# Modulation's products move from TensorE to VectorE, with its weights transposed and its tiles spread further along the stream

## The chip, the cores and the metric

One core of a Trainium2 chip runs the whole program as one launch. The metric is the device time of that launch in microseconds (us). It has five engines with a queue each: TensorE (PE; its weight loads are listed as PEld), VectorE (DVE), ScalarE (ACT), GpSimd (POOL) and SyncE (SP), which here only issues DMAs.

## The reference, cut to what matters

Two transformer blocks run one after the other on 256 tokens of width 2048, all in float32. What the change touches is the adaptive modulation of the first block:

```
mod   = silu(c)     @ ada_w + ada_b        # ada_w: 2048 x 12288, c: one vector of 2048
mod_c = silu(c_ctx) @ ada_w + ada_b
sh1, sc1, g1, sh2, sc2, g2 = split(mod, 6)  # 2048 each
sh1c, sc1c, ...            = split(mod_c, 6)
z  = modulate(rmsnorm(x,  norm1_g), sh1,  sc1)  @ w_in
zc = modulate(rmsnorm(xc, norm1_g), sh1c, sc1c) @ w_in
x  = x + g1 * (concat(attn, rwkv) @ w_out)
x  = x + g2 * swiglu(modulate(rmsnorm(x, norm2_g), sh2, sc2), ffn_w1, ffn_w3, ffn_w2)
```

Of `mod_c` only its first third (shift 1 and scale 1) reaches the output. The second block projects a memory of 256 rows with `mem_n @ w_mem_kv`, 2048 to 2048 columns, twice; that product depends on nothing of the first block.

## The kernel before, in words

**One stream of weights.** Every weight matrix is cut into tiles of 512 rows by 256 columns, 512 KB each, laid on 128 partitions as 1024 values a row. `weight_stream` (L58) lists all tiles in the order in which they are used, 1016 of them "split" tiles and 192 "raw" tiles of modulation. SyncE (L2624 to L2636) loads tile j into slot j modulo 6 of the ring `raw`, once tile j-6 has been used up, in order.

**Split tiles.** A float32 product is made of three products of halves. ScalarE rounds the tile (`hi`, L1462); then `hi` is subtracted from the tile (`lo`) by VectorE for even tiles (L1946) and by GpSimd for odd ones (L2535). Both go to `whl`, a ring of 4 slots, free again when TensorE has multiplied the tile four places back. `split_ahead` (L425) queues these steps up to 3 tiles of the stream ahead of TensorE, raw tiles counted. TensorE multiplies at L992.

**Modulation.** Column group `nt` (48 of them, 256 columns each) takes 4 raw tiles. Both vectors, silu(c) and silu(c_ctx), stand in `sc16`, each column 16 times over, as stationary operand of 32 columns; TensorE streams the raw tile past it, 4 matmuls a tile, in float32 (L944, `ada_tile`; the profile counts 8 each, two per matmul). The sums lie on 128 PSUM partitions; ScalarE copies them to `part`, TensorE adds them and turns them with two small matmuls (L952, `ada_sum`), and VectorE adds the bias into `mod`. So one `mod` column holds one output column on each partition.

**The order.** `schedule` (L326) is the same program for all engines, each of which queues its own part: memory's first norm beside 16 raw tiles; memory's 64 split tiles with one raw tile behind each (`memory_kv`; products of `mem0`, `mem1`), beside the sums of squares of context and x; the norms of x and of the context; then `w_k`, `w_v` (16 tiles each), `w_wa`, `w_ka`, `w_va`, `w_q` (4 each of the first three, 4 of the last) with 3 or 2 raw tiles behind each; from there on no raw tile is left. Then come attention, the RWKV scan, `w_out`, the feed-forward part in three parts of 8, 8 and 6 steps j with 8 split tiles (`ffn1`, `ffn3`) each, and the second block. The norms need modulation's groups 0 to 15, `w_out` needs 16 to 23, the second norm 24 to 39, `ffn2` 40 to 47. Within a queue everything is in order; semaphores link the queues.

## Time and profile before

| what | value |
|---|---|
| median of 3 runs | 4066.92 us (4062.89 to 4071.34) |
| the profiled execution, its own time | 4049.6 us |
| its span, first to last instruction | 4047.8 us |
| granted TensorE clock, mean | 0.982 |
| PE busy | 3859.6 us (95%) |
| VectorE busy | 1772.3 us (44%) |
| GpSimd busy | 1373.7 us (34%) |
| modulation on TensorE (L944) | 1536 matmuls, 113.8 us busy, from 16.6 to 641 us |

The profile lists instructions by line, engine and shape with their busy time, the mean of one in ns, and the idle time in front of them with what ended it. A timeline row starts with the start time and the duration in us of a run of like instructions; "x8" is their count. Matmul ends are modelled, so the distance between two starts says more than the duration. PEclk is the granted clock, 1.0 at 2.4 GHz, 0.5 at 1.2 GHz. The rows come further down.

### The profile page before, as it was taken

What the parts mean: (1) busy time and instruction counts of PE and PEld (TensorE: products, weight loads), DVE (VectorE), ACT (ScalarE), POOL (GpSimd) and SP (SyncE); (2) the same over time, 40 slices, a digit from 0 to 9 for tenths busy, and PEclk for the clock granted to TensorE, in tenths of its full rate; (3) what the DMA queues carried; (4) which work ended last, traced back from release to release, by engine and by line L of the source; (5) the groups of instructions that cost most, each with busy time, mean ns of one, the idle gap of its engine ahead of it and who ended that gap; (6) DMA issues with size and microseconds to landing.
All of it is one profiled execution on the core that took longest, in us unless ns stands there. A gap on an engine that the chain in (4) does not pass through costs nothing.

```text
span 4047.8 us, 81819 instructions
## 1 busy us (share of the span) xinstructions
PE 3859.6 (95%) x35588; PEld 3337.7 (82%) x35588; DVE 1772.3 (44%) x2247; ACT 1597.6 (39%) x2028; POOL 1373.7 (34%) x632
## 2 busy tenths in 40 slices
PE   8999999989888899999998999999899999999998
PEld 5777777888886778888887888897788888888887
DVE  2242125566664664344445445435333443333443
ACT  3342224622112344444444444434344444444443
POOL 2331113100001345455453344444343334443343
PEclk9999999999999999999999999999899999999999
DMA  8887665100001445555553554454455555555543
GB/s 325 285 306 255 234 220 181 51 22 4 4 4 66 152 161 192 192 188 191 184 197 134 180 176 171 163 166 159 163 184 174 174 169 175 177 175 173 173 161 136
DMA packets 183124, 667.53 MB, mean 165 GB/s; under 512 B 20432, under 2 KB 20432, under 8 KB 182384
## 3 DMA queue, kind: packets, MB, share of 16 engines
q1 hardware_dynamic: 176544, 642.07, 46.8%
q10 hardware_dynamic: 4944, 16.03, 1.1%
q8 instruction: 283, 4.64, 0.4%
q0 software_dynamic: 1280, 4.20, 0.3%
q14 instruction: 73, 0.60, 0.0%
HBM read 653.82 MB, written 8.39 MB: 164 GB/s over the span
## 4 chain that ended last, share of the span: by engine, by line
PE 86%; DVE 4%; ACT 3%; issue 2%; DMA 2%; PEld 1%; POOL 1%; ACTq 0%; PEldq 0%; DVEq 0%; POOLq 0%; SPq 0%
PE ps L992 68%; PE ps L944 2%; PE ps L1236 2%; PE ps L1212 2%; PE ps L1148 1%; PE ps L1226 1%; PEld ps L992 1%; ACT whl L1462 1%; POOL whl L2535 1%; DVE whl L1946 1%; PE ps L1450 1%; PE ps L1434 1%; PE ps L1337 1%; PE ps L923 1%; DMA raw<-in_w_k 1%
## 5 line engine op out<-in xcount | busy, mean ns | idle before, releaser
L992 PE MATMUL ps<-halves,whl 128*128 128x256 f32 (+1 forms) x14752 | 2594.7, 336 | 62.9 <-POOL halves L2535 17.9
L992 PEld LDWEIGHTS ps<-halves,whl 128*128 128x128 f32 x14752 | 2241.8, 191 | 384.1 <-issue 87.1
L2535 POOL TENSOR_TENSOR whl<-raw,whl 128x1024 fp32r<-128x1024 f32 x508 | 1241.3, 2444 | 1849.1 <-ACT whl L1462 1849.0
L1462 ACT ACTIVATE whl<-raw 128x1024 fp32r<-128x1024 f32 x1016 | 1062.3, 1055 | 1096.3 <-PE ps L992 748.8
L1946 DVE TENSOR_TENSOR whl<-raw,whl 128x1024 fp32r<-128x1024 f32 x508 | 792.7, 1561 | 1380.2 <-ACT whl L1462 1379.9
L992 PE MATMUL ps<-whl,halves 128*128 128x256 f32 x2752 | 488.8, 336 | 0.1
L992 PEld LDWEIGHTS ps<-whl,halves 128*128 128x128 f32 x2752 | 416.7, 188 | 63.1 <-issue 9.2
L1462 ACT ACTIVATE work<-ps 128x512 f32<-128x512 f32 (+1 forms) x240 | 131.5, 550 | 295.4 <-PE ps L992 225.7
L2535 POOL TENSOR_TENSOR halves<-mix,halves 128x1024 fp32r<-128x1024 f32 (+1 forms) x16 | 27.7, 1736 | 549.5 <-ACT halves L1462 549.5
L1946 DVE TENSOR_TENSOR work<-work,ps 128x512 f32<-128x512 f32 x157 | 107.7, 686 | 128.3 <-ACT work L1462 127.5
L944 PE MATMUL ps<-raw,sc 128*32 128x256 f32 x1536 | 113.8, 393 | 2.9 <-DMA raw<-in_ada 2.9
L1212 PE MATMUL ps<-X,BT 64*64 64x64 f32 x2560 | 94.3, 220 | 5.0 <-issue 4.8
L1236 PE MATMUL ps<-Xt,T 64*64 64x32 f32 x2560 | 93.1, 219 | 3.5 <-issue 3.2
L1212 PEld LDWEIGHTS ps<-X,BT 64*64 64x64 f32 x2560 | 85.7, 136 | 8.6 <-issue 7.2
L1236 PEld LDWEIGHTS ps<-Xt,T 64*64 64x64 f32 x2560 | 85.7, 135 | 5.3 <-issue 4.0
L1462 ACT ACTIVATE xw<-xw,cols 128x384 f32<-128x384 f32 (+1 forms) x32 | 25.0, 780 | 150.0 <-DVE cols L1952 150.0
L1946 DVE TENSOR_TENSOR T<-ps,rwc 128x512 f32<-128x512 f32 x80 | 55.1, 688 | 59.0 <-PE ps L1212 59.0
L1226 PE MATMUL ps<-T,Xt 64*64 64x32 f32 x2048 | 73.5, 218 | 4.1 <-issue 3.9
L1462 ACT ACTIVATE work<-x 128x512 f32<-128x512 f32 (+1 forms) x40 | 28.8, 719 | 121.6 <-DVE x L1949 63.3
L1226 PEld LDWEIGHTS ps<-T,Xt 64*64 64x64 f32 x2048 | 69.2, 135 | 8.9 <-issue 7.5
L944 PEld LDWEIGHTS ps<-raw,sc 128*32 128x32 f32 x1536 | 35.9, 109 | 45.0 <-issue 31.3
L1462 ACT ACTIVATE R<-ps 128x1024 f32<-128x1024 f32 x8 | 8.2, 1025 | 159.1 <-PE ps L1258 135.9
(248 smaller groups left out, 2450.1 us busy)
## 6 DMA issues: line engine op xcount, KB each, us to landing
raw<-in_ffn SPq DMA_DIRECT2D x264, 512.0 KB, 4.3
raw<-in_ada SPq DMA_DIRECT2D x192, 512.0 KB, 4.6
raw<-in_w_kv SPq DMA_DIRECT2D x192, 512.0 KB, 3.6
raw<-in_w_in_b SPq DMA_DIRECT2D x160, 512.0 KB, 3.6
raw<-in_w_in_a SPq DMA_DIRECT2D x128, 512.0 KB, 3.6
raw<-in_mem SPq DMA_DIRECT2D x64, 512.0 KB, 5.4
raw<-in_w_out_a SPq DMA_DIRECT2D x48, 512.0 KB, 3.8
raw<-in_w_out_b SPq DMA_DIRECT2D x48, 512.0 KB, 4.1
```

The lines of the kernel that those rows point to most:

```text
L923: m = self.e.matmul(self.X(2)[:, 0:T], self.ones, self.work4[q][:, c, :], start=(q == 0 and c == 0), stop=(q == 3 and c == 3))
L944: m = self.e.matmul(self.G(b)[32 * g:32 * g + 32, 0:256], self.sc16[:, 32 * k:32 * k + 32], raw[:, g, :], start=(t.kg == 0), stop=(t.kg == ...
L992: p = self.e.matmul(o, x, y, start=bi not in begun, stop=final and kc == 3 and m == len(pairs) - 1, skip_group_check=True)
L1148: m = self.e.matmul(o[h, s, c, :], lhs(r, s, d, c), rhs(r, s, d, c), start=True, stop=True)
L1212: m = self.e.matmul(o[h, c, :], q["BT"][h, s, c, :], q["X"][h, s, c, :], start=True, stop=True)
L1226: m = self.e.matmul(o[h, c, :], q["Xt"][h, s, c, :], self.even(T1[h, s, c, :], lv), start=True, stop=True)
L1236: m = self.e.matmul(o[h, c, :], T1[h, s, c, :], self.odd(q["Xt"][h, s, c, :], lv), start=True, stop=True)
L1337: m = self.e.matmul(self.X(0)[:, 0:T], self.ones, sq[:, c, :], start=(n == 0 and c == 0), stop=(n == 7 and c == 1), skip_group_check=True)
L1434: m = self.e.matmul(b[:, w * gi:w * gi + w], qs[gi][:, c, 128 * qb:128 * qb + 128], ks[gi][:, c, 0:w], start=True, stop=True)
L1462: return self.e.activation(out, in_, func, **kw)
L1946: return self.e.tensor_tensor(out, a, b, op)
L2535: return self.e.tensor_tensor(out, a, b, op)
```

## The change

Of the 48 column groups only 8 (the even ones of 0 to 15) stay on TensorE (`BY_PE`). The other 40 go to VectorE. For those, the host lays ada_w out transposed (`adaT`): a tile has 128 output columns on the partitions and 1024 rows of the reduction along the free axis. Both vectors are loaded spread over all partitions (`c_rows`, 1 MB each), ScalarE and VectorE make silu of them (`silu`), and VectorE multiplies a tile by the vector and sums along the row in one `scalar_tensor_tensor` with an accumulator output (`ada_rows`, L2095 of the changed kernel). Groups below 16 need it a second time for c_ctx (L2091). Two small additions finish a group (`ada_columns`).

The order changes too: 4 raw tiles, not 16, stand ahead of memory's first tile; memory's first 48 tiles have 5 raw tiles per 4, its last 16 have 1 each; behind `w_k` come 2 instead of 3, behind `w_wa`, `w_ka`, `w_va` 1 instead of 2; 32 raw tiles (groups 40 to 47) move into steps 1 to 7 of the feed-forward part, for which silu(c) is loaded and made a second time (`reload_x`, `silu(1)`). Groups of TensorE and VectorE alternate up to group 15.

```diff
+BY_PE = range(0, 16, 2)
+MODULATION = [0, 2, 4, 1, 6, 3, 8, 5, 10, 7, 12, 9, 14, 11, 13, 15, *range(16, 48)]
+BESIDE_MEM = (1, 1, 1, 2)
+BESIDE_NORM = (1, 1, 1, 1)
+BESIDE = (("w_k", range(1, 4), 2), ("w_v", range(4), 2), ("w_wa", range(1), 1), ("w_ka", range(1), 1), ("w_va", range(1), 1), ("w_q", range(1), 2))
+BESIDE_FFN = (0, 5, 5, 5, 5, 5, 5, 2)
-BESIDE_NORM = (3, 3, 3, 3)
-BESIDE = (("w_k", range(1, 4), 3), ("w_v", range(4), 2), ("w_wa", range(1), 2), ("w_ka", range(1), 2), ("w_va", range(1), 2), ("w_q", range(1), 2))
...
-    names.extend(itertools.islice(modulation, 16))
-    for w in [(f"mem{lay}", n, kg) for lay in range(2) for n in range(8) for kg in range(4)]:
-        names += [w, next(modulation)]
+    names.extend(itertools.islice(modulation, 4))
+    for i, w in enumerate((f"mem{lay}", n, kg) for lay in range(2) for n in range(8) for kg in range(4)):
+        names += [w, *itertools.islice(modulation, BESIDE_MEM[i % 4] if i < 48 else 1)]
...
-            add("ffn1", [j])
-            add("ffn3", [j])
+            beside = itertools.islice(modulation, BESIDE_FFN[j] if k0 == 0 else 0)
+            for w in [(name, j, kg) for name in ("ffn1", "ffn3") for kg in range(4)]:
+                names += [w, *itertools.islice(beside, 1)]
...
+    def silu(self, again):
+        for t in range(1 if again else 2):
+            self.wait_ge("ld_c2" if again else "ld_c", t)
+            if t:
+                self.wait_ge("silu_v", ("rows", 0))
+            self.act(self.silu_half[again], self.silu_in[t], ACT.Tanh, scale=0.5).then_inc(self.sig("silu_s", ("rows", t + 2 * again)), 1)
...
+    def silu(self, again):
+        for t in range(1 if again else 2):
+            x = self.silu_in[t]
+            self.wait_ge("silu_s", ("rows", t + 2 * again))
+            self.stt(x, self.silu_half[again], 1.0, x, ADD, MUL).then_inc(self.sig("silu_v", ("rows", t + 2 * again)), 1)
+
+    def ada_rows(self, t, i):
+        f, k = divmod(t.kg, 2)
+        raw, x = self.raw_of(t), self.silu_in[0]
+        self.wait_ge(f"raw{t.j % NRAW}", t.j)
+        if t.nt < 16:
+            self.wait_ge("silu_v", ("rows", 1))
+            self.e.scalar_tensor_tensor(self.silu_half[0][:, 0:1024], raw, 0.5, self.silu_in[1][:, 1024 * k:1024 * k + 1024], MUL, MUL,
+                                        accum_out=self.row_sums(i)[:, k, f, 1:2]).then_inc(self.own(), 1)
+            self.wait_own()
+        self.wait_ge("silu_v", ("rows", 2 if t.nt >= 40 else 0))
+        self.e.scalar_tensor_tensor(raw, raw, 0.5, x[:, 1024 * k:1024 * k + 1024], MUL, MUL,
+                                    accum_out=self.row_sums(i)[:, k, f, 0:1]).then_inc(self.sig("ada_v", t.a), 1)
+        self.last_row = t.a
+
+    def ada_columns(self, nt, i):
+        n = 2 if nt < 16 else 1
+        r = self.row_sums(i)[:, :, :, 0:n]
+        dst = self.mod[:, 4 * nt:4 * nt + 4].rearrange("p (f t) -> p f t", t=2)[:, :, 0:n]
+        b = self.cst("ada_b", 96)[:, 2 * nt:2 * nt + 2].unsqueeze(2).to_broadcast([128, 2, n])
+        self.wait_ge("ada_v", self.last_row)
+        self.tt(dst, r[:, 0], r[:, 1], ADD).then_inc(self.own(), 1)
+        self.wait_own()
+        self.tt(dst, dst, b, ADD).then_inc(self.sig("mod_v", nt), 1)
...
                 if old.kind == "raw":
-                    self.wait_ge("ada_mm", old.a)
+                    self.wait_ge("ada_mm" if old.name == "ada" else "ada_v", old.a)
```

What VectorE has queued, at three places. First, in memory's product, where a group that now belongs to VectorE passes. Before, `mod<-ps` adds a bias, `whl<-raw,whl` is the low half of a split tile, `work<-work,ps` collects a product of memory:

```order
L1946 TENSOR_TENSOR mod<-ps,const 128x4
L1946 TENSOR_TENSOR work<-work,ps 128x512
L1946 TENSOR_TENSOR whl<-raw,whl 128x1024 x2
L1946 TENSOR_TENSOR mod<-ps,const 128x4
L1946 TENSOR_TENSOR work<-work,ps 128x512
```

Now, for one such group (`c_70` is silu(c_ctx), `mix` silu(c), `ch` takes a product that nobody reads):

```order
L1997 TENSOR_TENSOR whl<-raw,whl 128x1024
L2091 SCALAR_TENSOR_TENSOR ch,cols<-raw,c_70 128x1024
L2095 SCALAR_TENSOR_TENSOR raw,cols<-raw,mix 128x1024
L2091 SCALAR_TENSOR_TENSOR ch,cols<-raw,c_70 128x1024
L2095 SCALAR_TENSOR_TENSOR raw,cols<-raw,mix 128x1024
L2091 SCALAR_TENSOR_TENSOR ch,cols<-raw,c_70 128x1024
L2095 SCALAR_TENSOR_TENSOR raw,cols<-raw,mix 128x1024
L1997 TENSOR_TENSOR mod<-ps,const 128x4
L1997 TENSOR_TENSOR whl<-raw,whl 128x1024
L2091 SCALAR_TENSOR_TENSOR ch,cols<-raw,c_70 128x1024
L2095 SCALAR_TENSOR_TENSOR raw,cols<-raw,mix 128x1024
L1997 TENSOR_TENSOR mod<-cols 128x4
```

Between two low halves stand up to six instructions of 1024 values where nothing of that size stood. Second, VectorE beside `w_v`, before:

```order
L1946 TENSOR_TENSOR whl<-raw,whl 128x1024
L1946 TENSOR_TENSOR mod<-ps,const 128x4
L1946 TENSOR_TENSOR whl<-raw,whl 128x1024
L1946 TENSOR_TENSOR mod<-ps,const 128x4
L1949 SCALAR_TENSOR_TENSOR vT<-ps,const,vT 128x2x255 x4
```

and now:

```order
L2095 SCALAR_TENSOR_TENSOR raw,cols<-raw,mix 128x1024 x2
L1997 TENSOR_TENSOR whl<-raw,whl 128x1024
L2095 SCALAR_TENSOR_TENSOR raw,cols<-raw,mix 128x1024 x2
L1997 TENSOR_TENSOR mod<-cols 128x2
L1997 TENSOR_TENSOR mod<-mod,const 128x2
L2000 SCALAR_TENSOR_TENSOR vT<-ps,const,vT 128x2x255 x4
```

Each tile of `w_v` brings two instructions of 1024 values along. Third, VectorE in the feed-forward part (the first rows are the gate's two steps and the low halves), before:

```order
L1946 TENSOR_TENSOR work<-work,ps 128x512
L1949 SCALAR_TENSOR_TENSOR work<-work 128x512
L1946 TENSOR_TENSOR whl<-raw,whl 128x1024 x2
L1946 TENSOR_TENSOR work<-work,ps 128x512
L1949 SCALAR_TENSOR_TENSOR work<-work 128x512
```

and now, in a step with 5 raw tiles:

```order
L1997 TENSOR_TENSOR work<-work,ps 128x512
L2000 SCALAR_TENSOR_TENSOR work<-work 128x512
L1997 TENSOR_TENSOR whl<-raw,whl 128x1024
L2095 SCALAR_TENSOR_TENSOR raw,cols<-raw,mix 128x1024
L1997 TENSOR_TENSOR whl<-raw,whl 128x1024
L1997 TENSOR_TENSOR work<-work,ps 128x512
L2000 SCALAR_TENSOR_TENSOR work<-work 128x512
L1997 TENSOR_TENSOR whl<-raw,whl 128x1024
L2095 SCALAR_TENSOR_TENSOR raw,cols<-raw,mix 128x1024 x2
```

They stand between the low halves on which TensorE waits.

## Rows read from the trace of the kernel before

**Rows 1.** The page, busy time by engine and in 40 slices

```profile
PE 3859.6 (95%) x35588; PEld 3337.7 (82%) x35588; DVE 1772.3 (44%) x2247; ACT 1597.6 (39%) x2028; POOL 1373.7 (34%) x632
```

**Rows 2.** Stretches: us, busy (count) by engine, PEclk, DMA share, GB/s

```profile
50.00:100.00 50.00, 50.00 (x344) 36.90 (x345) 10.93 (x14) 16.22 (x20) 17.04 (x10) 1.00 0.91 332
41.00:292.10 251.10, 250.45 (x1656) 186.97 (x1656) 68.36 (x99) 94.72 (x120) 84.27 (x47) 0.99 0.85 302
298.39:619.50 321.11, 318.35 (x2048) 233.88 (x2052) 75.00 (x116) 73.20 (x107) 53.95 (x24) 0.99 0.68 238
1482.20:1504.40 22.20, 22.20 (x130) 19.58 (x129) 10.70 (x8) 10.54 (x13) 11.44 (x5) 1.00 0.59 197
```

**Rows 3.** Timeline of PE, memory's product: four tiles, four raw tiles

```profile
199.92 0.61 PE L952 MATMUL ps<-const,work 128*128 128x2 f32 x4
200.39 3.03 PE L992 MATMUL ps<-halves,whl 128*128 128x256 f32 x16
203.34 0.64 PE L944 MATMUL ps<-raw,sc 128*32 128x256 f32 x8
203.91 3.09 PE L992 MATMUL ps<-halves,whl 128*128 128x256 f32 x16
...
214.60 0.61 PE L952 MATMUL ps<-const,work 128*128 128x2 f32 x4
```

**Rows 4.** Timeline of PE: memory's tiles 1, 3 and 49; w_k's first product

```profile
41.02 5.41 PE L992 MATMUL ps<-halves,whl 128*128 128x256 f32 x16 [3.08 <-issue]
...
50.47 3.05 PE L992 MATMUL ps<-halves,whl 128*128 128x256 f32 x16
...
234.38 3.03 PE L992 MATMUL ps<-whl,halves 128*128 128x256 f32 x16
...
298.39 7.32 PE L992 MATMUL ps<-halves,whl 128*128 128x512 f32 x24 [1.33 <-DVE halves L1949]
```

**Rows 5.** Timeline of PE: tiles of w_k, w_v, w_va, w_q

```profile
383.28 5.69 PE L992 MATMUL ps<-halves,whl 128*128 128x512 f32 x24 [0.32 <-POOL whl L2535]
391.00 5.76 PE L992 MATMUL ps<-halves,whl 128*128 128x512 f32 x24
...
449.79 5.74 PE L992 MATMUL ps<-halves,whl 128*128 128x512 f32 x24
455.46 1.07 PE L944 MATMUL ps<-raw,sc 128*32 128x256 f32 x16
...
598.86 6.01 PE L992 MATMUL ps<-whl,halves 128*128 128x256 f32 x48
...
643.43 4.63 PE L992 MATMUL ps<-halves,whl 128*128 128x256 f32 x24
```

**Rows 6.** VectorE's 1024-value instructions with two operands in SBUF: min/median/max ns

```profile
L1949 DVE SCALAR_TENSOR_TENSOR u<-u,Pinv x8: 1219/1221/1222, 835.2 to 1192.5; 128x1024 f32<-128x1024 f32 x8
```

**Rows 7.** Timeline: a low half on VectorE between two on GpSimd

```profile
1488.11 2.40 POOL L2535 TENSOR_TENSOR whl<-raw,whl 128x1024 fp32r<-128x1024 f32 x1
1488.78 2.81 DVE L1946 TENSOR_TENSOR whl<-raw,whl 128x1024 fp32r<-128x1024 f32 x1 [2.67 <-ACT whl L1462]
...
1490.87 2.98 POOL L2535 TENSOR_TENSOR whl<-raw,whl 128x1024 fp32r<-128x1024 f32 x1 [0.36 <-ACT whl L1462]
```

**Rows 8.** Groups by shape: a read of an accumulator, a table load, memory's collecting step

```profile
L1462 ACT ACTIVATION_READ_ACCUMULATOR hbl<-hbl,cols 128x1 f32 x32 | 6.1, 192 | 0.0
L1462 ACT ACT_TABLE_LOAD x24 | 30.8, 1283 | 1.2 <-PEq L2835 0.7
L1946 DVE TENSOR_TENSOR work<-work,ps x157: 670/687/691, 58.5 to 3859.7; 128x512 f32<-128x512 f32 x157
```

**Rows 9.** Timeline of ACT at the start; of VectorE before the feed-forward part

```profile
9.90 1.06 ACT L1462 ACTIVATE work<-hal 128x1024 f32<-128x1024 f32 x1 [0.21 <-DMA hal<-in_memT]
...
31.77 0.42 ACT L1462 ACTIVATE halves<-tm 128x256 fp32r<-128x256 f32 x1 [0.45 <-DVE tm L1949]
...
1431.02 1.75 DVE L1982 RECIPROCAL rst<-rst 128x256 f32<-128x256 f32 x1 [0.48 <-ACT rst L1462]
```

**Rows 10.** Stretch with the granted clock low, columns as in rows 2

```profile
41.00:47.00 6.00, 5.97 (x25) 4.53 (x25) 0.91 (x1) 2.40 (x3) 2.37 (x1) 0.56 0.90 363
```

More of the change, by code:

```diff
@@ L25 @@
     [f"raw{i}" for i in range(NRAW)]
[L26 to L27 removed]
+    + ["hi", "lo_v", "lo_g", "mm", "ada_mm", "ada_v"]
+    + [f"ld_mem{i}" for i in range(4)] + ["ld_const", "ld_c", "ld_c2", "ld_ctx", "ld_x", "ld_attn", "ld_rwkv", "ld_gup", "ld_x2", "ld_ret", "ld_x3", "ld_dil"]
     + ["ld_dec0", "ld_dec1", "st_x", "st_out"]
@@ L110, in weight_stream @@
     for j, (name, nt, kg) in enumerate(names):
-        kind = {"ada": "raw", "w_gd": "tail"}.get(name, "split")
+        kind = {"ada": "raw", "adaT": "raw", "w_gd": "tail"}.get(name, "split")
         out.append(Tile(j, name, nt, kg, 160 if name == "w_gd" else 256, kind, n, a))
@@ L329, in schedule @@
         rest(self.squares(0))
-        run_all((self.normed(0, 0, "HB"), 2), (limited(modulation, 16), 1))
+        run_all((self.normed(0, 0, "HB"), 5), (limited(modulation, 4), 1))
         for r in (None, 1, 2):
-            run_all((limited(memory, 16), 1), (limited(modulation, 16), 1), (self.squares(r) if r else iter(()), 1))
+            if not r:
+                self.silu(0)
+            run_all((self.after(limited(memory, 16), modulation, BESIDE_MEM), 1), (self.squares(r) if r else iter(()), 1))
         self.modulation()
@@ L369, in schedule @@
         self.root_of_sums(3)
+        self.silu(1)
         for part, (k0, k1) in enumerate(((0, 4), (4, 8), (8, 11))):
@@ L374, in schedule @@
                 if j:
-                    rest(chain(gate, value))
+                    run_all((chain(gate, value), 1), (limited(modulation, BESIDE_FFN[j] if part == 0 else 0), 1))
                 else:
@@ L403, in shift, with after, row_sums @@
         return {1: self.mods[:, 0, 1, :], 2: self.mods[:, 0, 0, :], 3: self.mods[:, 3, 0, :]}[k]
-    def ada_all(self):
-        for nt in range(48):
-            yield from self.ada(nt)
+    def after(self, g, other, counts):
+        counts = itertools.cycle(counts)
+        for _ in g:
+            rest(limited(other, next(counts)))
+            yield
+    def ada_all(self):
+        before = None
+        for i, nt in enumerate(MODULATION):
+            for kg in range(4):
+                if nt in BY_PE:
+                    t = self.next_tile("ada", BY_PE.index(nt), kg)
+                    self.ada_tile(t)
+                else:
+                    t = self.next_tile("adaT", nt, kg)
+                    self.ada_rows(t, i)
+                if before and kg == 0:
+                    self.ada_part(*before)
+                if before and kg == 2:
+                    self.ada_sum(before[0])
+                    before = None
+                if kg == 3:
+                    if nt in BY_PE:
+                        before = (nt, t.a)
+                    else:
+                        self.ada_columns(nt, i)
+                yield
+    def row_sums(self, i):
+        return self.cols[:, 8 * (i % 4):8 * (i % 4) + 8].rearrange("p (k f t) -> p k f t", k=2, f=2)
     def ev_lora(self, job):
@@ L438, in hi_lo @@
         return self.A("wh")[:, t.n % NW, 0:4 * t.w], self.A("wl")[:, t.n % NW, 0:4 * t.w]
-    def ada(self, nt):
-        for kg in range(4):
-            self.ada_tile(self.next_tile("ada", nt, kg))
-            if nt not in (0, 16) and kg == 0:
-                self.ada_part(nt - 1)
-            if nt not in (0, 16) and kg == 2:
-                self.ada_sum(nt - 1)
-            if nt in (15, 47) and kg == 3:
-                self.ada_part(nt)
-                self.ada_sum(nt)
-            yield
     def part(self, nt):
-        return self.parts[nt % 2]
+        return self.parts[nt // 2 % 2]
     def ada_bank(self, nt):
-        return (4, 5, 7)[nt % 3]
+        return (4, 5, 7)[nt // 2 % 3]
     def norm_tm(self, k, c):
@@ L2621, in schedule @@
                 self.e.dma_start(dst[:, 4 * q:4 * q + 4, :], io[src][:, 4 * q:4 * q + 4, :]).then_inc(self.sig(name, q, 16), 16)
+            if t.j == 6:
+                for i in range(2):
+                    self.e.dma_start(self.silu_in[i], io["c_rows"][i]).then_inc(self.sig("ld_c", i, 16), 16)
             if t.j == 146:
```

52 lines of the change are left out of this document (33 added, 19 removed).

## The prediction

> **What bounds the kernel now.** I read the busy times first: PE is busy for 95% of the span, VectorE for 44%, GpSimd for 34% [rows 1]. So time that leaves PE is worth having, if nothing else becomes late. Then the stretches: during memory's product (41 to 292 us) PE is busy for 250.45 of 251.10 us and from `w_k` to `w_va` for 318.35 of 321.11 [rows 2]. Modulation lies on the path nearly everywhere. What the reader is to see in the same rows is the company: in memory's product DMA already moves 302 GB/s, with 332 GB/s at a share of 0.91 in the fullest 50 us, which I take for the ceiling. Then the PE timeline gives prices. A raw tile takes 203.91 - 203.34 = 0.57 us, a group's closing pair 200.39 - 199.92 = 0.47 us, a memory tile 203.34 - 200.39 = 2.95 us, and four memory tiles with four raw ones and a pair 214.60 - 199.92 = 14.68, that is 3.67 us for one [rows 3]. Removing 160 raw tiles and 40 pairs frees 160 x 0.57 + 40 x 0.47 = 110 us of PE. The sum below asks how much of it arrives.
>
> **What VectorE takes over.** 32 tiles (groups 1, 3, ... 15) are done twice and 128 once: 192 instructions. The trace has no instruction with an accumulator on VectorE. The nearest is a `scalar_tensor_tensor` of 1024 values with both operands in SBUF: 1.22 us [rows 6]. Reading an accumulator costs ScalarE 0.19 us more [rows 8]. Back to back VectorE overlaps some 0.1 us, so I take 1.25 us, with 1.1 and 1.4 as ends. The page "Vector Engine (DVE) Microarchitecture Reference" of the Trainium skill ("Points that are easy to get wrong") says that this shape with two float32 sources in SBUF runs at half throughput, since no port is left to read the accumulator back. Without an accumulator the 1.22 us already contradict it; with one, no row here can tell. It would make about 2.4 us, and is a rival below.
>
> **VectorE and GpSimd take turns.** At 1488.78 a low half on VectorE takes 2.81 us: it ends 1.08 us after GpSimd's, which began first, ended (1488.11 + 2.40 = 1490.51). GpSimd's next, begun at 1490.87, takes 2.98 us and ends 2.26 us after VectorE's [rows 7]. So where both have two SBUF operands their times add: 1.1 us for VectorE's low half, 2.25 for GpSimd's. This is what I expect to eat most of the gain, for GpSimd's half is a load on VectorE that its 44% does not show.
>
> **Start.** Memory's first product starts at 41.02, the third at 50.47 [rows 4]. Now only 4 raw tiles stand ahead, and the first product can follow the norm at about 28 us. But ScalarE's silu stands behind the norm, whose last half ends at 32.2 [rows 9], and a split: about 34 us, a table load 1.3, a tanh of 2048 values 2.1 (twice the 1.06 of 1024), VectorE's 2.2, a second tanh 2.1, the third tile's two halves behind a further 2.2: the third product starts near 45.5. That is 5 us earlier, less 2 us because PE has waited and finds the low clock, at which the first product took 5.41 us [rows 4, 10]: **-3** (-5 to +2).
>
> **Alternating groups, memory tiles 3 to 38.** A VectorE group passes 3.2 memory tiles (5 raw per 4). It costs VectorE 8 x 1.25 = 10.0, 1.6 low halves 1.8, GpSimd's 1.6 in between 3.6, collecting 0.8 x 0.69 [rows 8] = 0.55, small adds 0.5: 16.5 us. A TensorE group costs PE 3.2 x 2.95 + 4 x 0.57 + 0.47 = 12.2 us. With no overlap of the two kinds a pair takes 28.7 us, 4.5 a tile. With perfect overlap DMA binds: 9 tiles of 0.524 MB per 4 memory tiles at 332 GB/s are 14.2 us, 3.55 a tile. Following one pair: PE gets the low half behind the third VectorE tile at about 12 us and has caught up 14 us later, after 6 memory tiles, when the ring, held up by raw tiles that wait for PE, lets the next group in: 24.5 us for 6, 4.1 a tile. (4.1 - 3.67) x 36 = **+15** (-4 to +30).
>
> **Groups 11, 13, 15 in a row**, 9.6 tiles: 16.5 / 3.2 = 5.15 us a tile, (5.15 - 3.67) x 9.6 = **+14** (-1 to +20).
>
> **Memory's last 16 tiles**, beside x's norm: before, (292.1 - 234.38) / 16 = 3.61 us each [rows 2, 4]. Now each has VectorE's 1.25 + two norm steps 0.8 + half a low half 0.55 + 0.25 for the rest, and GpSimd's 1.1: 3.95. **+5** (-6 to +10). Up to here memory's product gets slower by 31 us, although PE has less to do in it.
>
> **w_k to w_q.** Before, from 298.39 to 643.43 [rows 4, 5], 345 us. A tile of `w_k` is 391.00 - 383.28 = 7.7 us, of which the product takes 5.7; of `w_v` (455.46 - 449.79) 5.67 plus raw tiles; of `w_va` about 5.93 [rows 5]. VectorE and GpSimd per `w_v` tile: 2.5 + 0.55 + 0.75 (shifts) + 0.1 + 1.1 = 5.0 us, below 5.7: PE binds. Four `w_k` tiles beside the context's norm 30 us (VectorE binds, as now), then 36 x 5.7 = 205, 4 x 5.93 = 24, rotations 1.6; the 4 `w_q` tiles have 3 tiles of DMA each, 1.57 MB at 332 GB/s = 4.74, taken as 4.9: 20. With 3 for odd stalls 283.6: **-61** (-66 to -45).
>
> **Second silu.** A table load, a tanh (3.4 us) and VectorE's 2.2 stand between the root and the norm in front of the feed-forward part, where only the reciprocal's 1.75 us [rows 9] overlaps: **+4** (0 to +6). Loading c again is hidden by x's own reload.
>
> **Feed-forward.** A step j takes 22.20 us, all PE [rows 2]. VectorE and GpSimd now need: low halves 4 x 1.1 and 4 x 2.25, gate steps 4 x 0.65, GpSimd's half of the gate's result 1.15, and 5 x 1.2 for raw tiles: 23.2 us. 1 us over, in 6.4 steps, plus jitter, for a raw tile between two split tiles also uses up a place of the three that the splits run ahead: **+8** (0 to +20). DMA has 13 tiles in 22 us, 307 GB/s, below the ceiling.
>
> **Sum.** -3 + 15 + 14 + 5 - 61 + 4 + 8 = -18. Against the profiled execution's own 4049.6 us that is 4031.6; the median shown, 4066.9, stands 17 us higher, and I carry the difference: 4049 us. About 0.2%, 8 us, is what a measurement can tell from no change here.
>
> **Rivals.**
> *The turns are mostly hidden* (0.2). GpSimd's halves fall where VectorE waits for DMA or reads PSUM, and DMA sets memory's pace. For it: VectorE is busy 68.36 of 251 us there [rows 2]. Against it: in a VectorE group 16.5 us stand against 11.4 of DMA, and the ring has 6 slots. Memory then ends 14 us early and feed-forward costs nothing: -14 - 61 + 2 = -73, 3994 us.
> *TensorE falls to its low clock in memory's product* (0.2), the one that ends slower. PE waits some 2 to 3 us in every VectorE group, and after such waits rows show the clock at 1.2 GHz: 0.56 mean over 41 to 47, a product at 5.41 instead of 3.03 us [rows 3, 4, 10]. Three products at the low clock behind each of the 8 groups cost 8 x 3 x 2.4 = 58 us less what hides behind VectorE, say half to two thirds: +35, 4084 us. It decides from +26 on, about 11 slow products that nothing hides.
> *The accumulator halves VectorE's rate* (0.08). 80 such instructions in memory's product x 1.2 = 96 us; in the 28 tiles with two raw tiles 7.4 against 5.7, 48 us; feed-forward 32 x 1.2 = 38: +180, 4230 us.
> *The change does not take the products from PE*: the diff and the queues exclude it; no chance.
> The forecast itself has 0.47, and 0.05 is left for what I don't see.
>
> **How the numbers follow.** The forecast case alone spans about -45 to +12, most of it under -8. Faster: 0.2 plus six to seven tenths of 0.47, and a little of the rest: 0.53. Same: 0.17. Slower: most of the clock case, all of the accumulator's, a seventh of the forecast's: 0.30. The range reaches from the hidden case to above the clock case: 3985 to 4102 us; left out are mainly the accumulator and the far ends.
>
> **What would show it.** In the profile after: L2095 and L2091 at 1.2 to 1.4 us alone and longer beside GpSimd; `w_k`'s first product at about 329 us rather than 298; PE idle behind low halves of VectorE in memory's product, with memory tiles at 5 us in the last VectorE groups; `w_k` and `w_v` tiles 5.7 us apart; `w_q`'s end 30 us earlier than now; feed-forward steps of 23 us. I am wrong if memory's product ends before 292 us (then the turns were hidden), if the clock column falls under 0.9 there, or if L2095 takes over 2 us without GpSimd beside it.

## The result, and the profile after

| | before | changed kernel |
|---|---|---|
| median | 4064.9 us of 4 (4060.5 to 4071.34) | 4097.91 us of 4 (4089.65 to 4111.13) |
| ratio, 95% interval | | 1.0083 [1.0051, 1.0115] |
| profiled span | 4047.8 us | 4087.8 us |
| mean granted clock | 0.982 | 0.969 |

The change makes the kernel slower, by 0.8%. The prediction had 4049 us and gave "slower" 3 in 10. All medians and ratios here are of executions in the same, faster state; four executions of the kernel before, which took 5463 to 18839 us beside the last three experiments, are left out. The busy times of the profile after:

```profile
PE 3789.9 (93%) x34148; PEld 3318.7 (81%) x34148; DVE 2085.1 (51%) x2674; ACT 1590.6 (39%) x1993; POOL 1391.0 (34%) x632
```

Against [rows 1], PE lost 69.7 us of busy time (110 us of products left it, and what stayed ran at a lower mean clock than before) and VectorE got 312.8 more. Everything was moved as planned; the time did not follow. VectorE's tiles in the after profile, with min/median/max ns (`raw` is the tile, `mix` and `c` the vectors):

```profile
L2095 DVE SCALAR_TENSOR_TENSOR raw<-raw,mix x160: 1209/1220/3434, 72.2 to 1641.5; 128x1024 f32<-128x1024 f32 x160
L2095 DVE DVE_READ_ACCUMULATOR raw<-raw,mix x160: 72/81/86, 73.3 to 1642.6; 128x1 f32 x160
L2091 DVE SCALAR_TENSOR_TENSOR ch<-raw,c x32: 1162/1218/3406, 70.9 to 267.2; 128x1024 f32<-128x1024 f32 x32
```

The median is that of [rows 6] to the nanosecond, and reading the sum back is an instruction of 0.08 us of its own. The long ones, up to 3.43 us, stand beside GpSimd, like the low halves of [rows 7].

**Where the 40 us between the two spans are.** Four events in ScalarE's queue mark the stretches: the first evacuation of `w_k` into `xk` (ScalarE's copy of a finished product out of PSUM), the first square of `xk` (just behind `w_q`), the first gate step of the feed-forward part, and the recall of memory's product, where the second block begins. Before, the first start of each is 330.0, 713.5, 1465.1 and 2198.4 us; after, it is the first number behind the durations in these rows (the tile views of `xk` and of `work`):

```profile
L1503 ACT ACTIVATE xk<-ps,tsr x8: 679/686/690, 376.3 to 445.2; 128x512 f32<-128x512 f32 x8
L1503 ACT ACTIVATE sq<-xk,const x8: 711/714/716, 700.1 to 738.7; 128x512 f32<-128x512 f32 x8
```

```profile
L1503 ACT ACTIVATE halves<-work x22: 632/634/636, 1452.5 to 2147.0; 128x512 fp32r<-128x512 f32 x22
L1906 ACTq DMA_DIRECT2D work<-mem_keep x16: 326/450/455, 2238.3 to 2906.4; - x16
```

| stretch | before | after | difference | predicted |
|---|---|---|---|---|
| start, memory's product, first four tiles of w_k | 330.0 | 376.3 | +46.3 | +31 |
| w_k to w_q | 383.5 | 323.8 | -59.7 | -61 |
| attention, scan, w_out, second silu | 751.6 | 752.4 | +0.8 | +4 |
| feed-forward part | 733.3 | 785.8 | +52.5 | +8 |
| second block | 1849.4 | 1849.5 | +0.1 | 0 |

The gain beside `w_k` and `w_v` came in full, and was lost again on either side of it. The stretches after, columns as in [rows 2]:

```profile
41.00:292.10 251.10, 206.72 (x1147) 163.31 (x1145) 160.19 (x216) 77.20 (x90) 77.92 (x39) 0.91 0.74 268
...
300.00:350.00 50.00, 33.13 (x147) 26.73 (x145) 42.36 (x64) 16.72 (x25) 13.72 (x8) 0.82 0.70 243
```

```profile
1470.00:1650.00 180.00, 149.84 (x786) 125.89 (x786) 117.72 (x122) 64.44 (x74) 71.50 (x31) 0.95 0.63 230
```

In the feed-forward part no engine is full: PE is busy for 149.84 of 180 us, VectorE for 117.72, GpSimd for 71.50, and DMA moves 230 GB/s, where the fullest stretch of [rows 2] has 332. In memory's product DMA moves less than before too, 268 against 302 GB/s. Engines that all wait, and memory that is not asked for: something holds the ring.

**The hold, in one place.** The timeline of the changed kernel near its first gate steps, all engines (SPq is SyncE's queue; its row begins where the first of its DMAs is issued):

```profile
1455.55 3.42 DVE L2095 SCALAR_TENSOR_TENSOR raw<-raw,mix 128x1024 f32<-128x1024 f32 x1
...
1458.91 1.22 DVE L2095 SCALAR_TENSOR_TENSOR raw<-raw,mix 128x1024 f32<-128x1024 f32 x1
1459.01 0.33 SPq L2716 DMA_DIRECT2D raw<-in_adaT  x1
1459.43 0.39 SPq L2716 DMA_DIRECT2D raw<-in_ffn  x1
...
1460.58 8.25 SPq L2716 DMA_DIRECT2D raw<-in_ffn  x4
1463.80 1.06 ACT L1503 ACTIVATE whl<-raw 128x1024 fp32r<-128x1024 f32 x1 [8.73 <-DMA raw<-in_ffn]
1464.96 1.22 DVE L1997 TENSOR_TENSOR whl<-raw,whl 128x1024 fp32r<-128x1024 f32 x1 [4.83 <-ACT whl L1503]
1466.10 1.22 DVE L2095 SCALAR_TENSOR_TENSOR raw<-raw,mix 128x1024 f32<-128x1024 f32 x1
...
1466.33 4.18 PE L1033 MATMUL ps<-halves,whl 128*128 128x256 f32 x12 [4.76 <-DVE whl L1997]
```

VectorE is idle for 4.83 us ahead of a low half, although the raw tile whose product starts at 1466.10 was loaded long before: SyncE had issued its load at 1443.69. That product stands behind the low half in VectorE's queue, for `split_ahead` queues low halves up to three tiles of the stream ahead, but `ada_rows` is called where TensorE's program has come to, so at its own place. The low half waits for ScalarE, and ScalarE for a tile that is still on its way (8.73 us). That tile's load was issued at 1459.43, late, because SyncE goes in order and stood from 1445.11 to 1459.01: it waited for the slot of another raw tile, whose late product began at 1455.55 and took 3.42 us. So, where VectorE makes the low half of tile j+3, the product of tile j stands behind it, the load of tile j+6 waits for that product, and so it waits until tile j+3 has landed. The ring of 6 slots works like a shorter one. What SyncE waited for in 1470 to 1650 us of this kernel (us in total, times, the longest):

```profile
SPq L2716 <- DVE raw L2095: 137.5, 28, 11.7
SPq L235 <- POOL whl L2613: 6.2, 4, 3.3
SPq L235 <- DVE whl L1997: 3.0, 4, 1.0
```

Before, with the modulation on TensorE, SyncE waited for raw products too (392.6 us between 100 and 600 us), but in TensorE's queue these stood behind products of earlier tiles of the stream only.

The **order theory** says that this queueing costs most of what was lost. The **work theory** says it is the time of VectorE and GpSimd, which take turns, whatever the order. The **clock** (0.91 instead of 0.99 in memory's product) could be either's consequence or a cause by itself.

### The profile page after: what moved, and what is told of

Read it like the earlier page. It is cut to its first block, busy times and chain, and to the rows that moved or that the text cites. A ratio compares the mean times of both kernels' runs of the same rounds, so it can differ in the third digit from the quotient of the medians.

```text
span 4087.8 us, 79247 instructions
## 1 busy us (share of the span) xinstructions
PE 3789.9 (93%) x34148; PEld 3318.7 (81%) x34148; DVE 2085.1 (51%) x2674; ACT 1590.6 (39%) x1993; POOL 1391.0 (34%) x632
## 4 chain that ended last, share of the span: by engine, by line
PE 73%; DVE 11%; DMA 5%; ACT 4%; issue 3%; POOL 2%; PEld 1%; SPq 0%; ACTq 0%; DVEq 0%; PEldq 0%; POOLq 0%
PE ps L1033 58%; DVE raw L2095 3%; DMA raw<-in_mem 2%; ACT whl L1503 2%; DVE whl L1997 2%; PE ps L1253 2%; PE ps L1277 2%; POOL whl L2613 1%; PE ps L1267 1%; PEld ps L1033 1%; PE ps L1189 1%; DMA raw<-in_ffn 1%; DVE tm L2000 1%; ACT work L1503 1%; PE ps L1491 1%
## 5 line engine op out<-in xcount | busy, mean ns | idle before, releaser
L1033 PE MATMUL ps<-halves,whl 128*128 128x256 f32 (+1 forms) x14752 | 2620.0, 338 | 153.1 <-POOL whl L2613 46.3
L1033 PEld LDWEIGHTS ps<-halves,whl 128*128 128x128 f32 x14752 | 2267.4, 193 | 475.6 <-issue 168.1
L2613 POOL TENSOR_TENSOR whl<-raw,whl 128x1024 fp32r<-128x1024 f32 x508 | 1256.9, 2475 | 1878.9 <-ACT whl L1503 1878.7
L1997 DVE TENSOR_TENSOR whl<-raw,whl 128x1024 fp32r<-128x1024 f32 x508 | 781.3, 1538 | 1213.0 <-ACT whl L1503 1212.7
L1033 PEld LDWEIGHTS ps<-whl,halves 128*128 128x128 f32 x2752 | 424.9, 192 | 92.5 <-issue 35.9
L2095 DVE SCALAR_TENSOR_TENSOR raw<-raw,mix 128x1024 f32<-128x1024 f32 x160 | 237.7, 1504 | 3.5 <-DMA raw<-in_adaT 2.2
L1503 ACT ACTIVATE work<-ps 128x512 f32<-128x512 f32 (+1 forms) x200 | 116.0, 582 | 256.9 <-PE ps L1033 205.9
L1277 PEld LDWEIGHTS ps<-Xt,T 64*64 64x64 f32 x2560 | 85.3, 135 | 11.5 <-issue 10.7
L1503 ACT ACTIVATE R<-ps 128x1024 f32<-128x1024 f32 x8 | 8.2, 1024 | 160.5 <-PE ps L1299 136.2
L2000 DVE SCALAR_TENSOR_TENSOR work<-work 128x512 f32<-128x512 f32 x60 | 47.1, 785 | 34.5 <-ACT work L1503 33.7
```

The lines of the kernel that those rows point to most:

```text
L1033: p = self.e.matmul(o, x, y, start=bi not in begun, stop=final and kc == 3 and m == len(pairs) - 1, skip_group_check=True)
L1277: m = self.e.matmul(o[h, c, :], T1[h, s, c, :], self.odd(q["Xt"][h, s, c, :], lv), start=True, stop=True)
L1503: return self.e.activation(out, in_, func, **kw)
L1997: return self.e.tensor_tensor(out, a, b, op)
L2000: return self.e.scalar_tensor_tensor(*a)
L2095: self.e.scalar_tensor_tensor(raw, raw, 0.5, x[:, 1024 * k:1024 * k + 1024], MUL, MUL, accum_out=self.row_sums(i)[:, k, f, 0:1]).then_inc( ...
```

## The experiments

The kernel before ran beside each group of experiments, on the same chip as they, with medians of 4058.73 (the first four), 4064.43 (the next four) and 4068.13 us (the last three). The chips of the groups differ, so between groups the ratios to before are compared rather than the times.

### VectorE's products in the order of the stream

```diff
             if TILES[j].kind != "raw":
                 self.split_tile(TILES[j])
+            elif TILES[j].name == "adaT":
+                self.ada_ahead(TILES[j])
...
+    def ada_ahead(self, t):
+        i = MODULATION.index(t.nt)
+        self.ada_rows(t, i)
+        if t.kg == 3:
+            self.ada_columns(t.nt, i)
```

(and the calls in `ada_all` are gone.)

> VectorE's modulation products are queued in the order of the stream, as far ahead as the low halves, instead of behind the low half of a tile up to three places further on; nothing else changes. Order theory (a raw tile's ring slot comes free late because its product stands in VectorE's queue behind a low half whose tile has not landed and which itself waits for a slot): feed-forward steps fall from 27 to 33 us to 22 to 25, memory's product gets 10 to 40 us shorter, the total 4020 to 4055 us. Work theory (VectorE's and GpSimd's times add up to more than a step): the same work in another order, total within 15 us of the change's 4098.

Measured: 4020.72 us (4006.12 to 4023.72), ratio to before 0.9891 [0.9855, 0.9928]. With a few lines that remove no work, the slower kernel is 1.1% faster than the kernel before. From the changed kernel's span to this one's (4016.6) are 71.2 us: 27.6 up to `w_k`'s first evacuation (348.7), 16.9 from there to `w_q`, 26.1 in the feed-forward part. SyncE's waits in the same 180 us of the feed-forward part (1430 to 1610 here):

```profile
SPq L2721 <- DVE raw L2100: 57.3, 27, 3.0
SPq L235 <- DVE whl L2002: 44.7, 31, 3.3
SPq L235 <- POOL whl L2618: 40.7, 15, 6.4
```

The longest wait for a raw product is 3.0 instead of 11.7 us. In total SyncE waits nearly as long as in the changed kernel, 144 against 148 us, and it waited 157 us in 180 of the feed-forward part before: in a ring that runs full waiting is ordinary, and the total tells nothing. What tells is who waits for the loads. ScalarE's waits for tiles on their way, 1450 to 1600 us, in the changed kernel and in this one:

```profile
ACT whl L1503 <- DMA raw<-in_ffn: 72.1, 25, 9.1
```

```profile
ACT whl L1508 <- DMA raw<-in_ffn: 15.5, 9, 3.4
```

The seven steps that have raw tiles take 171.3 us; before it was 154.1, in the changed kernel 206.9. PE and the clock came back by themselves:

```profile
1430.00:1610.00 180.00, 171.90 (x963) 146.89 (x962) 140.33 (x133) 75.66 (x86) 95.75 (x38) 1.00 0.76 259
```

In this part the clock of 0.95 was the waits' consequence, not their cause. In memory's product it rose only from 0.91 to 0.94, where waits remain.

### Without raw tiles in the feed-forward part

```diff
-BESIDE_NORM = (1, 1, 1, 1)
-BESIDE = (("w_k", range(1, 4), 2), ("w_v", range(4), 2), ("w_wa", range(1), 1), ("w_ka", range(1), 1), ("w_va", range(1), 1), ("w_q", range(1), 2))
-BESIDE_FFN = (0, 5, 5, 5, 5, 5, 5, 2)
+BESIDE_NORM = (3, 3, 3, 3)
+BESIDE = (("w_k", range(1, 4), 3), ("w_v", range(4), 2), ("w_wa", range(1), 2), ("w_ka", range(1), 2), ("w_va", range(1), 2), ("w_q", range(1), 2))
+BESIDE_FFN = (0, 0, 0, 0, 0, 0, 0, 0)
```

(with the counts in `schedule` to match, and without the second load and silu of c.)

> The 32 raw tiles beside the feed-forward part go back to where they stood before (3 beside w_k, 2 beside w_wa, w_ka, w_va, 3 per tile beside the context's norm), and the second silu goes; memory's product stays as in the change. Both theories: feed-forward steps back to 22.2 us, 50 us less there. The dense part pays for it: 5 to 10 us beside the norm, and 12 tiles of w_k at 6.3 us instead of 5.7 (four tiles of DMA, 2.1 MB at 332 GB/s), 15 to 25 us in all. Total 4060 to 4075 us, no faster than the kernel before.

Measured: 4085.34 us, ratio 1.0056 [1.0036, 1.0076]. The feed-forward part is back at 734.4 us, steps at 22.2, so the raw tiles alone had cost it the 52 us. But `w_k`'s first evacuation comes at 388.7, 12 us later than in the changed kernel, and `w_k` to `w_q` takes 350.4 instead of 323.8. 39 of the 52 us are paid elsewhere, more than was expected. SyncE's waits between 300 and 700 us here are led by the same cause:

```profile
SPq L2714 <- DVE raw L2093: 267.8, 122, 9.4
```

### Products over 64 of 1024 values, old order

```diff
-        self.e.scalar_tensor_tensor(raw, raw, 0.5, x[:, 1024 * k:1024 * k + 1024], MUL, MUL,
+        self.e.scalar_tensor_tensor(raw[:, 0:64], raw[:, 0:64], 0.5, x[:, 1024 * k:1024 * k + 64], MUL, MUL,
```

(L2091 likewise. The sums leave out 15 of 16 values, so the outputs are not the right ones.)

> The change with every modulation product on VectorE over 64 instead of 1024 values of a row (most of modulation's sums is left out); queues, waits and DMAs stay. Work theory: VectorE's load is nearly gone, so memory's tiles go at DMA's 3.6 us, feed-forward steps at 22.2, total 3965 to 3990 us. Order theory: what a raw tile waits for stays, so feed-forward steps stay above 24.5 us and the total above 4010.

Measured: 4011.21 us, one run. `w_k`'s first evacuation comes at 325.1, 51.2 us before the changed kernel's, so in memory's product the work matters. But the feed-forward steps are still 24.4 to 29.5 us, the part takes 784.3, and SyncE still waits for the products, which now take 0.22 us:

```profile
SPq L2716 <- DVE raw L2095: 121.3, 18, 12.0
```

There the work is not what costs.

### GpSimd's low halves over 64 values

```diff
-            self.tt(lo, self.raw_of(t), hi.bitcast(F32), SUB).then_inc(self.sig("lo_g", t.n), 1)
+            w = 64 if t.j < GATE or t.name in ("ffn1", "ffn3") else 4 * t.w
+            self.tt(lo[:, 0:w], self.raw_of(t)[:, 0:w], hi.bitcast(F32)[:, 0:w], SUB).then_inc(self.sig("lo_g", t.n), 1)
```

(and a memset at the start, so that what is left out reads as zero.)

> The change with GpSimd's low halves over 64 instead of 1024 values in everything before w_out and in ffn1 and ffn3 (the rest of those low halves is left out). It takes away GpSimd's turns at VectorE's expense. If the turns are the loss: memory's product 40 to 55 us shorter, feed-forward steps 22 to 24 us, total 4000 to 4020. Order theory: memory 10 to 30 us shorter, feed-forward steps still 26 us or more, total above 4045.

Measured: 4036.89 us, one run: evacuation at 356.9 (-19.4), the feed-forward part 772.9 us, most of its steps with raw tiles at 26.5 to 27.1, all seven 183.5 instead of 206.9 us. So GpSimd's turns are part of what both stretches lost, 19 of 46 us up to the evacuation and 23 of 53 in the seven steps, if nothing else is changed; but the steps do not come near 22.2, and with the order right most of this is gone as well (171.3 us with GpSimd's work in full). The two causes overlap, so their shares don't add up.

### Stream order without raw tiles in the feed-forward part

> As e1_stream (VectorE's products of raw tiles queued where they stand in the stream), and in addition the 32 raw tiles of the feed-forward part are back beside w_k and what follows, as in the kernel before, and the second silu is gone. From e1_stream the feed-forward part should give back 25 us (759.7 us from its first gate step to the second block, 734.4 in e2_noffn) with its steps at 22.2. What the 32 tiles cost beside w_k tells the theories apart. Order theory: in stream order a tile of w_k with 3 raw tiles is bound by DMA, 4 x 0.524 MB at 332 GB/s = 6.3 us instead of 5.4, 12 tiles +11, the norm's four tiles +6: 4020.7 - 25 + 17 = 4013 us. Work theory (VectorE's and GpSimd's times add up, whatever the order): e2_noffn paid 27 us in w_k and 12 ahead of it for the same move, so 4020.7 - 25 + 39 = 4035 us.

Both edits above together. Measured: 4018.67 us, ratio 0.9891 [0.9872, 0.991], the same ratio as stream order alone: the 32 tiles cost as much beside `w_k` as in the feed-forward part. The third tile behind each tile of `w_k` costs 7.5 us up to the evacuation (356.2) and 4.9 from there to `w_q` (311.8 for 306.9), 12.4 where the order theory had 17 and the work theory 39. In the old order the same tiles had cost 39. The feed-forward part gave back 13.2 us, not 25: my 25 compared two profiles in which TensorE had different paces, 12 us apart over this part (the last section). So 13 is what VectorE's work costs there.

### All groups of two vectors back on TensorE

```diff
-BY_PE = range(0, 16, 2)
-MODULATION = [0, 2, 4, 1, 6, 3, 8, 5, 10, 7, 12, 9, 14, 11, 13, 15, *range(16, 48)]
+BY_PE = range(16)
+MODULATION = [*range(48)]
```

(with `part` and `ada_bank` by nt again, and group 15 closed in its own last step.)

> As e1_stream, but all groups 0 to 15 stay on TensorE, one after the other, so that the products which VectorE must make twice (64 instructions of 1.2 us) are gone from memory's product and TensorE has 8 x (4 x 0.57 + 0.47) = 22 us more to do there. Work theory (what memory's product still loses in e1_stream, w_k's first evacuation at 348.7 instead of 330.0, is VectorE's and GpSimd's time): TensorE binds again, the evacuation comes at 325 to 330, and the whole takes 4020.7 - 20 = 4000 us. Clock or DMA theory (VectorE's work is covered once the order is right, and the loss is TensorE's clock or the ring): TensorE's 22 us come on top in part, evacuation at 350 to 360, the whole 4022 to 4032 us.

The products are queued in stream order here too. Measured: 4003.27 us, ratio 0.9854 [0.9834, 0.9874]. The total is the work theory's; the evacuation, at 339.1, is 9.6 us earlier than in stream order alone and not at 325 to 330. So the groups that VectorE makes twice cost some 10 us more than the 22 us of TensorE that they save (by the total some 15, though the two intervals overlap, and they are of different chips), and another 10 us up to the evacuation are lost to something else. In memory's product PE is busy for 231.60 of 251.10 us again (250.45 before), at a clock of 0.99:

```profile
41.00:292.10 251.10, 231.60 (x1540) 174.92 (x1536) 92.36 (x122) 92.55 (x116) 80.35 (x44) 0.99 0.86 305
```

### Stream order with products over 64 values

> As e1_stream, but VectorE's products go over 64 of the 1024 values, so 40 groups of modulation are wrong sums and the outputs with them; loads, order and waits are the same. Order theory: e3_tiny left the late queueing in place and its feed-forward steps stayed at 27 to 29 us without VectorE's work; with stream order they fall to 22 to 23, and the whole to 4011 - 7 x 5 = 3976 us. If VectorE's queue order were not what holds the ring, the steps stay at 27 and the whole at 4011. The distance from e1_stream to this kernel (some 45 us) is what VectorE's work still costs when the order is right: about 24 in memory's product (325.1 in e3_tiny against 348.7), 14 in the feed-forward steps.

Measured: 3967.87 us, one run. Feed-forward steps 22.2 to 22.6, 745.7 us for the part; evacuation at 313.7. PE waits for nothing between 1400 and 1580 us. With the third and the first experiment that makes a square (evacuation / feed-forward part, us):

| | queued where TensorE is | queued in stream order |
|---|---|---|
| full products | 376.3 / 785.8 | 348.7 / 759.7 |
| 64 values | 325.1 / 784.3 | 313.7 / 745.7 |

The changed kernel's 785.8 was measured at TensorE's faster pace (the last section), the other three at the slower, so the sums of the whole part can't be compared straight. The seven steps with raw tiles can, within 3 us (without raw tiles they take 154.1 us at one pace, 157.1 at the other): 206.9 and 171.3 us with full products, 194.0 and 156.7 with 64 values. There the order costs 36 to 39 us and the work 13 to 16. Up to the evacuation it is the other way round: the work costs 35 to 51 us, the order 11 to 28. Between the evacuation and `w_q` (323.8 and 306.9; 308.0 and 307.2) either alone gives back 16 to 17 us, and both together no more. So both theories hold: the order leads in the feed-forward part, the work in memory's product. The row of 64 values rests on one run each.

A side result: between 200 and 250 us of this kernel DMA moves 365 GB/s at a share of 0.96, so the 332 GB/s that the prediction took for the ceiling was none; [rows 10] already had 363 for 6 us. The page "Perfetto Trace Analysis" of the Trainium skill, in its section "Roofline", says that one active core can draw more than its share of 358 GB/s, up to what its 16 DMA engines carry; this stretch agrees.

```profile
200.00:250.00 50.00, 45.10 (x249) 37.80 (x247) 32.13 (x84) 19.81 (x24) 18.04 (x10) 0.97 0.96 365
```

### Memory's weights first, alone

The kernel before with this part of the change and nothing else:

```diff
-    names.extend(itertools.islice(modulation, 16))
-    for w in [(f"mem{lay}", n, kg) for lay in range(2) for n in range(8) for kg in range(4)]:
-        names += [w, next(modulation)]
+    names.extend(itertools.islice(modulation, 4))
+    for i, w in enumerate((f"mem{lay}", n, kg) for lay in range(2) for n in range(8) for kg in range(4)):
+        names += [w, *itertools.islice(modulation, BESIDE_MEM[i % 4] if i < 48 else 1)]
```

> The kernel before with one part of the change alone: 4 raw tiles stand ahead of memory's first tile instead of 16, and memory's first 48 tiles have 5 raw tiles per 4; modulation stays on TensorE. TensorE has as much to do as before, so only idle time of the start can go: memory's first product was at 41 us, after 16 raw tiles that took TensorE 9 us of 24. If weights and TensorE are what the start lacks, the first product comes at about 29 and w_k's first evacuation 5 to 12 us earlier than 330.0: 4050 us. If the ceiling of DMA (0.91 of its time at 332 GB/s) binds the start, since 5 raw tiles per 4 now load beside memory's first tiles, nothing is gained: 4059 us.

Measured: 4070.0 us, ratio 1.0021 [1.0004, 1.0039]: no gain. Memory's first product does start 12 us earlier, but slow and with nothing behind it:

```profile
29.05 5.46 PE L999 MATMUL ps<-halves,whl 128*128 128x256 f32 x16 [11.16 <-DVE whl L1953]
34.44 0.79 PE L951 MATMUL ps<-raw,sc 128*32 128x256 f32 x8
37.14 4.57 PE L999 MATMUL ps<-halves,whl 128*128 128x256 f32 x16 [1.91 <-ACT whl L1469]
...
66.29 3.06 PE L999 MATMUL ps<-halves,whl 128*128 128x256 f32 x16 [0.88 <-DVE whl L1953]
71.27 3.02 PE L999 MATMUL ps<-halves,whl 128*128 128x256 f32 x16 [0.81 <-POOL whl L2542]
```

Two products ran at the low clock, waits for low halves follow that the kernel before does not have, and the evacuation of `w_k` comes at 339.0 instead of 330.0. The 12 us won at the start are lost again before `w_k`, and 9 more. Neither expectation foresaw a loss in this stretch, and what the 9 us are made of was not pursued.

### The kernel that is left when the losing parts are out

The next takes the all-groups-on-TensorE kernel and gives memory's stage its old order (16 raw tiles ahead, one behind each), with silu made of c alone, its load moved from tile 6 to tile 40 of the stream and the silu into the second quarter of memory's product:

```diff
-    names.extend(itertools.islice(modulation, 4))
-    for i, w in enumerate((f"mem{lay}", n, kg) for lay in range(2) for n in range(8) for kg in range(4)):
-        names += [w, *itertools.islice(modulation, BESIDE_MEM[i % 4] if i < 48 else 1)]
+    names.extend(itertools.islice(modulation, 16))
+    for w in [(f"mem{lay}", n, kg) for lay in range(2) for n in range(8) for kg in range(4)]:
+        names += [w, next(modulation)]
...
-        for t in range(1 if again else 2):
+        for t in range(1):
```

> As e6_stream_pe16, but memory's stage as in the kernel before: 16 raw tiles ahead of memory's first tile and one behind each; silu is made of c alone, beside memory's second quarter, since no group of VectorE needs c_ctx. It asks what memory's weights first are worth with the VectorE work gone from there. e8_order_only took 278.0 us from its first memory product to w_k's (29.05 to 307.07) where the kernel before takes 257.4 (41.02 to 298.39), 9 us later in all. Theory 'the earlier order costs': w_k's first evacuation at 328 to 332 instead of 339.1, and the whole 4003.3 - 8 = 3995 us. Theory 'the order is neutral, e8 was noise': within 3 us of 4003.

Measured: **3999.62 us** (3989.14 to 4008.02), ratio 0.9835 [0.9814, 0.9857]. The evacuation is at 328.4, as forecast, 10.7 us earlier; the order and the smaller, later silu were changed together here, but the order alone had cost 9 us above. Yet of that little shows in the total (8 expected; 0.9854 to 0.9835, with overlapping intervals).

Then the raw tiles of the feed-forward part back beside `w_k` as well, by the edit of BESIDE shown above:

> As e9_mem_as_before, and in addition no raw tiles in the feed-forward part and no second silu: of the change only the products of groups 16 to 47 on VectorE remain, in stream order. e5_stream_noffn against e1_stream says that the 32 tiles cost the same in either place (4018.7 and 4020.7, different chips): then this comes out within 5 us of e9_mem_as_before, about 3993. If VectorE's 14 us in the feed-forward part are worth more than what three tiles behind each tile of w_k cost, it is 5 to 15 us slower than e9; the other way round 5 to 10 faster.

Measured: 4003.18 us, ratio 0.9839 [0.982, 0.9857]: as expected, no difference from the one before. So the part of the change that touches the feed-forward part, with its second silu and second load, is worth nothing. Not pursued: from `w_q` to the first gate step these two kernels take 761.7 and 759.3 us, where the kernel before takes 751.6.

And that kernel with the queueing of the changed one:

```diff
+                    self.ada_rows(t, i)
...
-            elif TILES[j].name == "adaT":
-                self.ada_ahead(TILES[j])
```

> As e10_mem_as_before_noffn, but VectorE's products queued where the changed kernel has them (at their place in TensorE's program, behind low halves of up to three tiles further on). Order theory: with 3 raw tiles behind each tile of w_k the late product holds slots, and TensorE waits: 20 to 50 us slower than e10 (e2_noffn was 66.7 us slower than e5_stream_noffn, 32 of it by w_k's first evacuation and 28 from there to the end of w_v). Work theory: within 5 us of e10.

Measured: 4055.66 us, ratio 0.9977 [0.9959, 0.9996]; 52.5 us slower than the same work in stream order (just above the 20 to 50 that the order theory gave). The evacuation comes at 350.3 for 336.9, and `w_k` to `w_q` takes 358.5 for 312.8. Between 340 and 500 us, in stream order and then in the other:

```profile
340.00:500.00 160.00, 156.02 (x680) 126.84 (x680) 143.71 (x214) 38.64 (x43) 37.45 (x15) 1.00 0.86 316
```

```profile
340.00:500.00 160.00, 131.83 (x505) 105.06 (x506) 102.42 (x167) 28.15 (x31) 26.96 (x11) 0.88 0.71 250
```

680 matmuls against 505, with VectorE *less* busy where it is late. This pair tells most clearly for the order theory: one edit, no work changed, and a stretch in which the changed kernel, with 2 raw tiles behind each tile of `w_k` and not 3, had looked healthy. It also settles the clock for this stretch: by the same edit it goes from 1.00 to 0.88.

## Why the prediction was wrong

Against its own steps, in profiled time:

- **"Feed-forward ... +8 (0 to +20)" is the step that failed**: +52.5, outside its range, and enough by itself to turn -18 into +26. It added engine times (23.2 us a step) and compared them with TensorE's 22.2. As a sum of work that was fair: in stream order the part takes 759.7 us against 745.7 with the products shrunk, +14. Missing was the cost of the place in the queue, 36 to 39 us: the seven steps took 206.9 us where stream order takes 171.3, and the raw products were waited for up to 11.7 us. The text came near ("a raw tile between two split tiles also uses up a place of the three that the splits run ahead") and put it under jitter. The rows for it were there: the queue listing showed two raw products behind a low half, and the text said that SyncE loads slot j once tile j-6 is used up. I never asked which engine's queue frees a slot, and behind what that instruction stands.
- **Memory's terms, -3 + 15 + 14 + 5 = +31, measured +46.3.** Inside the sum of their ranges, but made up otherwise. In stream order the stretch is 18.7 us longer than before, less than my 31; that is what VectorE's and GpSimd's work and the start cost. The other 27.6 us are the order again, which no term had. In the start I had the first product right (about 28 us forecast, 29.28 measured, at the low clock) and the third (45.5, measured 45.89), but not that the early order loses what it won and 9 us more before `w_k`, as the run with the order alone shows. The sum also took 332 GB/s for DMA's ceiling, which is too low; it set no term of memory's product, only the far end of its range and the 20 us of `w_q`.
- **w_k to w_q, -61: -59.7.** The number came out by luck: the stretch was not yet bound by TensorE throughout: stream order took another 16.9 us out of it, 5 to 6 us each in `w_k`, in `w_v` and behind them, and made it -76.6, outside my range of -66 to -45. The saving was set too small and the queue's cost left out, and the two errors cancelled. That the term held with 2 raw tiles and would have failed with 3 (350.4 instead of 323.8) the prediction did not know.
- **Second silu, +4: +0.8**, within the range. In the three pairs of runs with and without it the stretch differs by 2.4 to 6.9 us, which also fits 4.
- **VectorE's instruction, 1.25 us: 1.22 plus 0.08 for the accumulator.** The rival that an accumulator halves the rate is out. The page "Vector Engine (DVE) Microarchitecture Reference" of the Trainium skill ("Points that are easy to get wrong") has this shape at half throughput; the 192 instructions measured here contradict it, and the measurement decides.
- **The rival "low clock"**, 0.2, gave 4084 and is nearest to the result in its number. Its observation was right (0.91 over memory's product, just above the 0.9 that I had named as a sign, and 0.82 from 300 to 350 us), but in the feed-forward part and beside `w_k` the clock was back at 1.00 with the order alone, so there it followed from the waits. What it costs in memory's product by itself no run separates. An estimate of the most it can be, from these rows: 0.91 instead of 0.99 over 251 us is 20 us of full-clock time. And it does not follow the time: with 64 values it is 0.97 in the old order and 0.95 in stream order, where the evacuation comes 11 us earlier. The rival "turns hidden" is out.
- The range, 3985 to 4102, held 4097.91; the likeliest case and its sign were wrong. That it held is luck: its upper end was set by the clock case, which is not what happened.

What I asked of the new profile did point to it: the w_k product at 346.57 instead of 329, steps of 25.4 to 33.5 instead of 23 us.

## What to carry to other kernels

When work moves to another engine, ask not only whether that engine has time, but what its new instructions free (a ring slot) and what stands ahead of them in its queue. Here an instruction that frees a slot stood behind one that waits for a load three places further on. That chains the loads to each other through the DMA queue, and the engines wait together with bandwidth to spare. Queue consumers in the order of the loads. And take a large change apart before judging it: here three of its four parts were worth nothing or less (doubled products, weights first, tiles in the feed-forward part), and the fourth, in the right order, was worth 1.6% (ratio 0.9839).

## What the runs showed of the hardware beyond that

TensorE's pace in the first block's feed-forward part differs between executions by 1.8% at the same granted clock of 1.00, and holds for that whole part. Two kernels of one chip and one job, stretch 1650 to 1700 us of the old-memory-order kernel and of the one without raw tiles, in a place where both do the same products with PE always busy:

```profile
1650.00:1700.00 50.00, 50.00 (x290) 44.15 (x290) 21.37 (x20) 22.11 (x25) 23.50 (x10) 1.00 0.59 185
```

```profile
1650.00:1700.00 50.00, 50.00 (x285) 43.41 (x284) 21.09 (x19) 21.40 (x24) 23.29 (x10) 1.00 0.57 184
```

290 or 285 matmuls, 22.2 or 22.6 us a step, 12 us over the part (734.4 against 746.5 in the two kernels without raw tiles there that differ in the order). The kernel before, the changed kernel and three others had the first, the other eight the second; each kernel has one profile. It does not belong to an execution as a whole: between 2960 and 3010 us, in the second block, the kernel before, the changed kernel and the one without raw tiles in the feed-forward part show 285 matmuls, all three of the faster kind in the first block, and the kernel before with memory's weights first shows 290, one of the slower kind. What sets it is open, and no run was made to tell; whether it accounts for the 17 us between the profiled execution of before and its median is not shown. Whoever compares single profiles here in the feed-forward part has to set off up to 12 us first.
